# One decoder step on one core: compressed keys from token pairs on 128 rows, first scores between the two compressions, sums of a pair of units in one copy

## The chip, the cores and the metric

The kernel runs on one core of a Trainium2 chip. The metric is the device time of one execution in microseconds (us), the median of three runs; lower is better. A core has the engines PE (TensorE, matrix products), DVE (VectorE), ACT (ScalarE), POOL (GpSimd) and SP (SyncE, which here only issues DMAs). They run their own instruction streams and meet at semaphores.

## The reference, cut to what matters

One step of a hybrid decoder for 1024 prompt tokens and 8 samples of 4 tokens, each sample with 256 cached tokens. One of its three head groups is sparse attention, in which each query also looks at *compressed* keys and values. They are made like this:

```python
CMP_LEN, CMP_STRIDE, CMP_HIDDEN, HEAD_DIM = 32, 16, 128, 64

def nsa_compress(rows, w1, w2, pe):          # rows: (batch, tokens, 64)
    n_cmp = (rows.shape[1] - CMP_LEN) // CMP_STRIDE + 1
    idx = jnp.arange(n_cmp)[:, None] * CMP_STRIDE + jnp.arange(CMP_LEN)[None, :]
    blocks = rows[:, idx] + pe
    h = jax.nn.gelu(jnp.einsum('bnld,ldh->bnh', blocks, w1))
    return jnp.einsum('bnh,hd->bnd', h, w2)

kc = nsa_compress(nkv[:, :, 0], cw1[0], cw2[0], cpe[0])
vc = nsa_compress(nkv[:, :, 1], cw1[1], cw2[1], cpe[1])
```

A window is 32 tokens long and windows start every 16 tokens: 63 for the prompt, 15 for each sample. Keys and values go through the same two layers with their own weights. The prompt attention then adds four outputs for each head and block of 128 queries: fox (forgetting attention), slc (selected blocks, here all of them), win (a window of 512) and cmp (the compressed keys).

## The kernel before

All data are float32. Large products run first (stages p1 and hgrn, to about 475 us of the span). Stage p2b projects keys and values of the prompt tile by tile: a first loop over nine token tiles for fox (512 columns), then a second for the sparse heads (400 columns, `token_tile`, L709). In the second loop PE turns each finished tile (`turn_sparse_keys`, L807) and DVE copies the three turned blocks out of PSUM (`sparse_keys_turned`, L1733, L1734, L1736): 128 rows hold keys (rows 0 to 63) and values (64 to 127) of the compression as `kcvc`, with tokens along the columns. After the last tile PE turns the cached tokens of the samples (L826, four banks of four blocks), ACT copies them out (L1378), and PE turns the last tile and the position table (L834).

Stage p3 makes the compressed keys and values. PE makes 32 products for the keys and 32 for the values (L845), in turn on rows 0 to 63 and 64 to 127, one for each position l in the window; its moving operand is every 16th column of `kcvc` from l on, 193 columns. DVE adds the bias (L1794 to L1798) and makes the gelu over all 366 columns (L1779 to L1789) with one Exp on ACT (L1393). PE makes four second products (L850 to L860), DVE copies their results (L1802 to L1811); the last of these copies is the event "KC ready".

Beside it ACT makes the log forget values and copies the queries (L1385, L1389); after the event "LF ready" (L1767) POOL issues 15 DMAs of outputs (L2250 to L2258).

Stage attn runs over 64 units d: 4 heads, 8 query blocks i, and for each (fox, slc) as an even d and (win, cmp) as an odd one. Each engine has its own loop written out by hand:

- PE (L938): `scores(d)` (L887), `transposes(d-2)` (L899), `values(d-3)` (L911 and L912 for even units, L924 and L926 for odd). Ahead of it, and at every 16th unit, `decay_rows` (L869).
- DVE (L1882): `scores(d)` adds the bias and takes the least value (L1853), `normalise(d-1)` (L1863 to L1869), and at even d `add_halves(d-3)` (L1878), which frees the bank of the sums. `decay_rows` (L1826) is a chain of eight steps.
- ACT (L1406): copies of the turned probabilities of d-2 (L1419), then two Exps of unit d (L1428). At even d the sums of unit d-3 are copied between the two Exps: L1403 copies the lower half to `other_half`, L1404 the fox output to `QT`.
- POOL adds the diagonal mask for each head (`foxdiag`, L2264, L2267); the DVE `scores` of even units wait for it.

PSUM has eight banks: ring "vec" of four (scores and decay rows, in the order in which they are asked for), three for turned probabilities and one for the sums. SP's queue is in order too: bias strips of heads 0 and 1 (L525, L526), the first layer's weights `w1c` (L532, L533, after the wait for the first loop of p2b), the 16 cached pages `KVT` (L544), and after "KC ready" the rest of the caches (L549 on).

## Time and profile before

| what | value |
|---|---|
| median of three runs | 1415.16 us (1415.08 to 1419.33) |
| the profiled execution | 1417.93 us, of which the span of the page is 1416.1 us |
| PE busy | 1274.9 us, 90% of the span |
| DVE, ACT, POOL busy | 51%, 30%, 13% |
| mean granted clock of PE | 0.951 |

In the rows below "busy" is the time in which an engine's instructions ran, and "granted clock" the share of TensorE's full clock (1.00 is 2.4 GHz, 0.50 is 1.2 GHz). A float32 product is shown as two instructions ("x2"). The chain of waits is followed back from the last instruction to what released each step.

### The profile page before, as it was taken

The page shows a single profiled execution, that of the slowest core. Times are in us where ns is not written, and L with a number is a line of the kernel's source. Part 1 is how long each engine was busy: PE and PEld are TensorE (multiplying, and loading weights), DVE is VectorE, ACT ScalarE, POOL GpSimd, SP SyncE. Part 2 cuts the span into 40 slices and gives each one's busy share as a digit, 9 for nine tenths or more (in the row PEclk, how much of TensorE's full clock was granted, in tenths as well). Part 3 has the DMA queues.
Part 4 walks back from the last instruction along what each step waited for, and adds up shares of the span by engine and source line. Part 5 has one row for each costly group of instructions (what it writes and reads, how often), then busy time and mean ns, then how long its engine had stood idle before and what let it go on. Part 6 is the DMA issues. An engine that isn't in the chain of part 4 may idle for free.

```text
span 1416.1 us, 19719 instructions
## 1 busy us (share of the span) xinstructions
PE 1274.9 (90%) x6966; PEld 760.1 (54%) x6966; DVE 724.3 (51%) x1693; ACT 419.3 (30%) x894; POOL 177.6 (13%) x209
## 2 busy tenths in 40 slices
PE   3699999999999999969998999999829999999966
PEld 1468787787877545645665665545323333333322
DVE  5526584665755101247787783344752443433339
ACT  2232242422321200226666773222201111111016
POOL 0003121031221000200000000000001222211132
PEclk9799999999999999968999999999958999999988
DMA  9812021030111204204100005410267978495856
GB/s 314 246 31 60 2 66 25 23 70 3 31 60 47 98 0 90 96 6 121 42 18 24 16 1 164 153 45 15 82 232 244 321 240 296 151 334 158 283 181 224
DMA packets 124360, 163.19 MB, mean 115 GB/s; under 512 B 29860, under 2 KB 98644, under 8 KB 124281
## 3 DMA queue, kind: packets, MB, share of 16 engines
q1 hardware_dynamic: 109960, 112.75, 26.2%
q0 software_dynamic: 14320, 49.41, 10.2%
q8 instruction: 48, 0.79, 0.2%
q14 instruction: 32, 0.25, 0.1%
HBM read 225.01 MB, written 36.45 MB: 185 GB/s over the span
## 4 chain that ended last, share of the span: by engine, by line
PE 75%; DVE 15%; DMA 3%; ACT 3%; issue 2%; POOL 1%; SPq 0%; DVEq 0%; POOLq 0%; ACTq 0%
PE act L680 16%; PE vec L1202 11%; PE vec L962 9%; PE vec L709 7%; PE vec L730 4%; PE act L899 4%; PE vec L887 4%; DMA arena<-x_rows,arena 2%; PE act L911 2%; PE act L1215 2%; PE vec L1215 2%; PE vec L845 1%; PE act L924 1%; PE vec L690 1%; DVE arena L1653 1%
## 5 line engine op out<-in xcount | busy, mean ns | idle before, releaser
L680 PE MATMUL act<-arena 128*128 128x352 f32 x768 | 239.3, 468 | 0.4 <-issue 0.4
L680 PEld LDWEIGHTS act<-arena 128*128 128x128 f32 x768 | 145.7, 193 | 77.1 <-issue 3.7
L1202 PE MATMUL vec<-arena 128*64 128x512 f32 x768 | 173.8, 605 | 2.8 <-issue 2.8
L962 PE MATMUL vec<-arena 128*128 128x512 f32 (+1 forms) x288 | 126.6, 594 | 1.1 <-DVE arena L1878 1.1
L1202 PEld LDWEIGHTS vec<-arena 128*64 128x64 f32 x768 | 54.4, 138 | 105.3 <-issue 105.0
L709 PE MATMUL vec<-arena 128*128 128x512 f32 (+1 forms) x256 | 99.9, 546 | 0.0
L2157 DVE TENSOR_SCALAR arena<-arena 128x256 f32<-128x256 f32 x24 | 7.1, 295 | 172.5 <-ACT arena L1521 172.5
L1428 ACT ACTIVATE arena<-arena 128x640 f32<-128x640 f32 (+15 forms) x128 | 82.3, 645 | 20.6 <-DVE arena L1853 20.3
L962 PEld LDWEIGHTS vec<-arena 128*128 128x128 f32 (+1 forms) x288 | 50.9, 180 | 68.4 <-issue 66.1
L1419 ACT COPY arena<-act 128x512 f32<-128x512 f32 (+11 forms) x176 | 63.4, 428 | 62.1 <-PE act L899 62.0
L1853 DVE CUSTOM_DVE_ANT_0 arena<-vec,arena 128x128 f32<-128x128 f32 (+6 forms) x168 | 68.8, 430 | 24.5 <-PE vec L887 15.6
L899 PE MATMUL act<-arena 128*128 128x128 f32 (+4 forms) x440 | 67.0, 290 | 14.5 <-DVE arena L1869 13.9
L887 PE MATMUL vec<-arena 64*128 64x512 f32 (+11 forms) x376 | 72.5, 469 | 3.2 <-DVE arena L1853 2.0
L709 PEld LDWEIGHTS vec<-arena 128*128 128x128 f32 x256 | 47.8, 190 | 44.9 <-issue 27.7
L1674 DVE COPY_PREDICATED arena<-arena,vec 128x512 f32<-128x512 int32 x64 | 44.5, 728 | 48.3 <-PE vec L730 46.4
L899 PEld LDWEIGHTS act<-arena 128*128 128x128 f32 (+4 forms) x440 | 47.7, 143 | 36.0 <-DVE arena L1869 22.3
L730 PEld LDWEIGHTS vec<-arena 128*128 128x128 f32 x512 | 61.9, 192 | 9.3 <-DVE arena L1657 3.2
L690 PE MATMUL vec<-arena 128*128 128x128 f32 (+1 forms) x576 | 65.3, 275 | 0.0
L690 PEld LDWEIGHTS vec<-arena 128*128 128x128 f32 (+1 forms) x576 | 64.5, 183 | 1.3
L730 PE MATMUL vec<-arena 128*128 128x128 f32 x512 | 62.7, 276 | 2.4 <-DVE arena L1657 2.4
L1521 ACT ACTIVATE arena<-vec 128x256 f32<-128x256 f32 x24 | 9.3, 386 | 167.0 <-PE vec L1202 167.0
L1297 ACT ACTIVATE arena<-act,arena 128x352 f32<-128x352 f32 x36 | 20.0, 555 | 127.4 <-PE act L680 127.4
(383 smaller groups left out, 1940.5 us busy)
## 6 DMA issues: line engine op xcount, KB each, us to landing
arena<-in_exp_w SPq DMA_DIRECT2D x144, 1024.0 KB
y_rows<-arena POOLq DMA_DIRECT2D x48, 256.0 KB, 4.8
arena<-in_w_in SPq DMA_DIRECT2D x16, 512.0 KB, 6.8
arena<-in_x_prompt SPq DMA_DIRECT2D x8, 512.0 KB, 9.2
x_spill<-arena POOLq DMA_DIRECT2D x8, 512.0 KB, 5.3
arena<-x_spill SPq DMA_DIRECT2D x8, 512.0 KB, 5.1
arena<-in_cache_fox_kv SPq DMA_DIRECT2D x16, 256.0 KB, 3.5
x_rows<-arena POOLq DMA_DIRECT2D x8, 512.0 KB, 2.9
```

The costliest lines, as they stand in the source:

```text
L680: last = mm(bk[:, 0:n], W[k % 2][:, c, m * P:(m + 1) * P], xT[:, c, a:a + n], start=c == 0, stop=c == NC - 1)
L690: last = mm(bk[:r, o:o + P], xT[:, c, t * P:t * P + r], W[h % 2][:, c, 3 * P:4 * P], start=c == 0, stop=c == NC - 1)
L709: last = mm(bk[:r, 0:width], xT[:, c, t * P:t * P + r], w[:, c, 0:width], start=c == 0, stop=c == NC - 1)
L730: last = mm(bk[:, c * P:(c + 1) * P], a[:, ch], b[:, ch], start=True, stop=True)
L887: mm(bk[:, 0:n], q[s, h, i * P:(i + 1) * P], k[:, 0:n], start=True, stop=True).then_inc(*E.filled("vec", *events))
L899: last = e.transpose(bk[:n, c * P:(c + 1) * P], score_tiles(d)[j][:, (a + c) * P:(a + c) * P + n], ident)
L962: last = mm(bk[:r], src, Wo[half][:, c, :], start=c == 0, stop=c == NC - 1)
L1202: last = mm(gu_bank[p][o], xgT[p][:, c, o], Wgu[:, slot, c, :], start=c == 0, stop=c == NC - 1)
L1215: last = mm(dn_bank[half][o], hT[p][:, f, o], Wd[:, slot, f, half * 512:(half + 1) * 512], start=f == 0, stop=f == 1)
L1419: e.copy(turned_tiles(d)[j][:w, a:a + k, :], bk[:w, 0:k * P].rearrange("p (c n) -> p c n", c=k)).then_inc(*E.drained("turned", ("pt", d, j)))
L1428: act(s, s, ACT.Exp, scale=-1.0, bias=sm_[:, least(i, kind, j):least(i, kind, j) + 1], accum_out=sm_[:, j:j + 1]).then_inc(*E.done(("exps" ...
L1853: ins = e.tensor_tensor_reduce(out=out, in0=in0, in1=bias, scale=1.0, scalar=prior, op0=ALU.add, op1=ALU.min, accum_out=sm_[:, col + m[j]: ...
```

## The change

1. `kcvc` is replaced by `tokens2`: rows 0 to 63 hold even tokens, rows 64 to 127 odd ones, for keys and values apart, so that the windows of one offset lie in neighbouring columns. The first layer is 16 products for the keys and 16 for the values, each over 128 rows and 193 neighbouring columns. Each turned block is copied out in four pieces (keys and values, even and odd), by DVE for the prompt, by ACT for the cached tokens.
2. The cached tokens are turned inside the second loop of p2b, after tiles 1, 3, 5 and 7; the position table after tile 0.
3. Keys and values of the compression are worked apart. PE's order is: hidden layer of the keys, `decay_rows(0)`, scores of unit 0, hidden layer of the values, second layer of the keys (one product), scores of units 1 and 2, second layer of the values, and on. DVE and ACT have matching orders; the compressed keys are copied out by ACT.
4. The sums of an odd unit are one ACT copy of 128 rows straight to `QT`, and DVE adds the last part from PSUM. ACT makes this copy ahead of both Exps of unit d.
5. SP's order: long strips, cached pages, `w1c` in four DMAs, then, after the wait for the second loop of p2b, the local strips of heads 0 and 1. The later cache loads wait for "VC ready".

```diff
-    kcvc, KVT = zk.take(NTOK), zk.take(DB * PAST, DB, NP)
+    tokens2, KVT = zk.take(NTOK + DB * PAST, 2, 8), zk.take(DB * PAST, DB, NP)
...
@@ sync
         load_strips(0)
         load_strips(1)
-        e.wait_ge(*E.at(("w_in used", 5)))
-        e.dma_start(w1c[0:64], I["nsa_cmp_w1"][0, 0].rearrange("l d x -> d l x")).then_inc(*E.moved("cmp_in"))
-        e.dma_start(w1c[64:128], I["nsa_cmp_w1"][0, 1].rearrange("l d x -> d l x")).then_inc(*E.moved("cmp_in"))
...
         for n in range(DB * NP):
             e.dma_start(KVT[:, n // NP, n % NP, :], nkp[page_of(n), :, 0:2].rearrange("a p k d -> p (a k d)")).then_inc(*E.moved("cmp_cache_in"))
-        e.wait_ge(*E.at("KC ready"))
+        e.wait_ge(*E.at(("w_in used", 5)))
+        for kv in range(2):
+            for odd in range(2):
+                src = I["nsa_cmp_w1"][0, kv].rearrange("(j two) d x -> two d j x", two=2)
+                e.dma_start(w1c[64 * odd:64 * odd + 64, kv], src[odd]).then_inc(*E.moved(f"cmp{kv}_in"))
         e.wait_ge(*E.at(("w_in used", 6)))
+        load_local_strips(0)
+        load_local_strips(1)
+        e.wait_ge(*E.at("VC ready"))
@@ tensor
         for t in range(NT):
             token_tile(t, W_nkvg, 400, 6)
+            if t == 0:
+                e.wait_ge(*E.at("pe_in"))
...
+                e.wait_ge(*E.at("cmp_cache_in"))
+            if t % 2 and t < 8:
+                turn_cached_keys(t - 1)
             if t >= 2:
                 turn_sparse_keys(t - 2)
+        turn_sparse_keys(7)
...
+        e.wait_ge(*E.at("pairs by act"))
+        e.wait_ge(*E.at("cmp_in"))
+        def hidden_values(kv):
+            e.wait_ge(*E.at(f"cmp{kv}_in"))
+            e.wait_ge(*E.at(("pairs by vec", kv)))
+            e.wait_ge(*E.free("vec"))
+            bk = E.bank("vec")
+            for j in range(16):
+                last = mm(bk[:, 0:WINDOWS], w1c[:, kv, j, :], tokens2[:, kv, j % 8, j // 8:j // 8 + WINDOWS], start=j == 0, stop=j == 15)
+            last.then_inc(*E.filled("vec"))
...
-        for l in range(32):
-            for kv in range(2):
-                s = slice(64 * kv, 64 * kv + 64)
-                last = mm(hidden_banks[kv][:, 0:WINDOWS], w1c[s, l, :], skew(kcvc[s, :], l, [16, WINDOWS]), start=l == 0, stop=l == 31)
...
+        hidden_values(0)
+        e.wait_ge(*E.at("LF ready"))
+        decay_rows(0)
         E.stage("attn")
-        e.wait_ge(*E.at("KC ready"))
...
         for d in range(n + 3):
+            if d == 1:
+                hidden_values(1)
+                compressed_keys()
+                e.wait_ge(*E.at("KC ready"))
...
+            if d == 4:
+                e.wait_ge(*E.at("VC ready"))
...
+            if d == 2:
+                compressed_values()
@@ scalar
-        def lower_sums(d):
+        def sums(d):
             h, i, _ = PAIRS[d]
             e.wait_ge(*E.full("summed"))
             bk = E.job("summed")
-            e.copy(other_half[64:128], bk[0:64, P:2 * P]).then_inc(*E.done(("other half", d)))
-            e.copy(QT[0:64, h, i * P:(i + 1) * P], bk[0:64, 0:P]).then_inc(*E.done(("fox output", d)))
+            e.copy(QT[:, h, i * P:(i + 1) * P], bk[:, 0:P]).then_inc(*E.done(("sums copied", d)))
         for it in range(n + 3):
+            if it == 1:
+                compressed_keys()
+                gelu_exp(1)
...
+            if it >= 4 and it % 2 == 0:
+                sums(it - 3)
...
-                    if j and it >= 3 and kinds[0] == "fox":
-                        lower_sums(it - 3)
@@ vector
+        def pairs_of(bk, n, at):
+            for kv in range(2):
+                turned = bk[64 * kv:64 * kv + 64, 0:n].rearrange("p (w r two) -> p two r w", r=8, two=2)
+                for odd in range(2):
+                    last = cp(tokens2[64 * odd:64 * odd + 64, kv, :, at // 16:(at + n) // 16], turned[:, odd])
+                    last.then_inc(*E.done(*([("pairs by vec", kv)] if odd else [])))
...
-            cp(kcvc[:, t * P:(t + 1) * P], bk[:, 0:P]).then_inc(*E.done())
+            pairs_of(bk, P, t * P)
...
-            e.wait_ge(*E.at(("other half", d)))
-            e.wait_ge(*E.at(("fox output", d)))
-            tt(QT[64:128, h, i * P:(i + 1) * P], bk[64:128, 0:P], other_half[64:128], ALU.add).then_inc(*E.drained("summed", ("halves added", d), "prompt attention done"))
+            e.wait_ge(*E.at(("sums copied", d)))
+            x = QT[64:128, h, i * P:(i + 1) * P]
+            tt(x, x, bk[0:64, P:2 * P], ALU.add).then_inc(*E.drained("summed", ("halves added", d), "prompt attention done"))
         n = len(PAIRS)
+        gelu_inner(0)
         decay_rows(0)
+        gelu_outer(0)
         for it in range(n + 3):
+            if it == 1:
+                normalise(0)
+                gelu_inner(1)
             if it < n:
                 scores(it)
+                if it == 1:
+                    gelu_outer(1)
+                if it == 2:
+                    compressed_values()
```

`gelu_inner(kv)` and `gelu_outer(kv)` are the steps of the old gelu ahead of and behind its Exp, each for 183 of the 366 columns.

## Rows read from the trace of the kernel before

**Rows 1.** Chain of waits around stage p3: start us, us, what.
```profile
586.60 21.18 PE vec L845 x128
611.66 2.45 DVE arena L1787
624.46 2.00 POOL arena L2264
```

**Rows 2.** Ten-us stretches: length, busy PE, PEld, DVE, ACT, POOL, granted clock, DMA, GB/s.
```profile
610.00:620.00 10.00, 4.50 (x26) 3.79 (x27) 5.41 (x9) 0.51 (x1) 0.00 (x0) 0.50 0.00 0
630.00:640.00 10.00, 9.97 (x43) 5.31 (x40) 5.98 (x33) 5.80 (x24) 0.00 (x0) 0.50 0.09 9
```

**Rows 3.** Groups by form: busy us, mean ns of one, idle before.
```profile
L845 PE MATMUL vec<-arena 64*128 64x193 f32 x128 | 21.2, 501 | 0.9 <-DVE arena L1757 0.9
L709 PE MATMUL vec<-arena 128*128 128x400 f32 x112 | 38.6, 499 | 0.0
```

**Rows 4.** Timeline of the end of p2b: start us, us, engine, line, instruction.
```profile
583.24 1.91 PE L826 MATMUL act<-arena 128*128 128x128 f32 x16
582.99 1.12 DVE L1745 TENSOR_TENSOR arena<-vec,arena 32x100 f32<-32x100 f32 x4 [0.45 <-PE vec L699]
585.51 0.29 DVE L1733 COPY arena<-vec 128x128 f32<-128x128 f32 x1 [0.54 <-PE vec L807]
```

**Rows 5.** Timeline beside and behind the 193-column products, columns as in rows 4.
```profile
589.30 3.88 ACT L1389 COPY arena<-arena 64x1024 f32<-64x1024 f32 x4
590.18 0.94 POOL L2250 DMA_DIRECT2D out_new_fox_kv_p<-arena  x1 [133.96 <-DVE arena L1772]
595.20 3.99 POOL L2258 DMA_DIRECT2D out_new_nsa_win_s<-arena x8
607.80 0.16 DVE L1794 COPY arena<-vec 128x1 f32<-128x1 f32 x1 [17.43 <-PE vec L845]
615.45 0.23 DVE L1802 COPY arena<-vec 64x63 f32<-64x63 f32 x1 [0.78 <-PE vec L850]
616.47 1.89 PE L860 MATMUL vec<-arena 128*15 128x64 f32 x16
621.30 0.29 DVE L1826 TENSOR_SCALAR arena<-vec 128x128 f32<-128x128 f32 x1 [2.23 <-PE vec L869]
626.48 0.29 DVE L1853 CUSTOM_DVE_ANT_0 arena<-vec,arena 128x128 f32<-128x128 f32 x1 [2.12 <-POOL arena L2264]
```

**Rows 6.** The same units of heads 0 and 2: DVE scores(d=3), PE decay_rows at d=8.
```profile
630.19 0.28 DVE L1853 CUSTOM_DVE_ANT_0 arena<-vec,arena 128x128 f32<-128x128 f32 x1
647.75 2.05 PE L869 MATMUL vec<-arena 128*128 128x128 f32 x16 [0.71 <-DVE arena L1853]
...
752.14 0.29 DVE L1853 CUSTOM_DVE_ANT_0 arena<-vec,arena 128x128 f32<-128x128 f32 x1
765.16 2.05 PE L869 MATMUL vec<-arena 128*128 128x128 f32 x16 [0.77 <-DVE arena L1853]
```

**Rows 7.** Timeline of a short even unit (d=36), columns as in rows 4.
```profile
756.05 0.26 ACT L1404 COPY arena<-act 64x128 f32<-64x128 f32 x1
756.45 0.29 DVE L1878 TENSOR_TENSOR arena<-act,arena 64x128 f32<-64x128 f32 x1 [0.46 <-ACT arena L1404]
```

**Rows 8.** Timeline of the longest even unit (d=30), columns as in rows 4.
```profile
736.75 1.18 ACT L1428 ACTIVATE arena<-arena 128x1024 f32<-128x1024 f32 x1
737.28 0.27 PE L926 MATMUL act<-arena 128*64 128x128 f32 x1
738.49 1.15 ACT L1428 ACTIVATE arena<-arena 128x1024 f32<-128x1024 f32 x1
740.35 0.15 DVE L1863 SCALAR_TENSOR_TENSOR arena<-arena 128x2 f32<-128x2 f32 x1
742.22 2.00 PE L899 MATMUL act<-arena 128*128 128x128 f32 x16 [0.87 <-DVE arena L1869]
```

**Rows 9.** DMA issues of 480 to 640 us: count, KB each, median us to landing.
```profile
arena<-strip_rows SPq DMA_DIRECT2D x2, 320.0 KB, 6.5
```

More of the change, by code:

```diff
@@ L47 @@
 STRIPW = SLCW + WINW
[L48 removed]
+HALF_GELU = NCMP + DB * NCMPS
+GELU = 2 * HALF_GELU
 WINDOWS = NTOK // 16 + 16 * DB - 1
@@ L1377, in _ @@
             bk = E.job("act")
-            e.copy(KVT[:, b:b + 2].rearrange("p b j n -> p (b j n)"), bk).then_inc(*E.drained("act", "KVT ready"))
+            at = (NTOK + b * PAST) // 16
+            for kv in range(2):
+                turned = bk[64 * kv:64 * kv + 64].rearrange("p (w r two) -> p two r w", r=8, two=2)
+                for odd in range(2):
+                    last = e.copy(tokens2[64 * odd:64 * odd + 64, kv, :, at:at + PAST // 8], turned[:, odd])
+                    last.then_inc(*(E.drained("act", "pairs by act") if kv and odd else E.done()))
         e.wait_ge(*E.at("gate logits"))
@@ L1390, in _, with gelu_exp, compressed_keys @@
         E.stage("p3")
-        def gelu_exp(n, tag):
-            e.wait_ge(*E.at((tag, "inner")))
-            act(gu[:, 0:n], gu[:, 0:n], ACT.Exp, scale=-1.5957691216057308).then_inc(*E.done((tag, "exp")))
-        gelu_exp(GELU, "cmp hidden")
+        def gelu_exp(kv):
+            u = gu[:, kv * HALF_GELU:(kv + 1) * HALF_GELU]
+            e.wait_ge(*E.at(("gelu inner", kv)))
+            act(u, u, ACT.Exp, scale=-1.5957691216057308).then_inc(*E.done(("gelu exp", kv)))
+        def compressed_keys():
+            e.wait_ge(*E.full("act"))
+            bk = E.job("act")
+            e.copy(KC[64:128, 0:NCMP], bk[64:128, 0:NCMP]).then_inc(*E.done())
+            e.copy(KCs[64:128, :], bk[64:128, NCMP:HALF_GELU]).then_inc(*E.drained("act", "KC ready"))
+        gelu_exp(0)
         E.stage("attn")
         n = len(PAIRS)
-        def lower_sums(d):
+        def sums(d):
             h, i, _ = PAIRS[d]
@@ L1773, in _, with gelu_inner @@
         e.reciprocal(GT[:, 8, :], GT[:, 8, :]).then_inc(*E.done())
-        def gelu(n, tag):
-            x, u = gx[:, 0:n], gu[:, 0:n]
+        def gelu_inner(kv):
+            o = kv * HALF_GELU
+            x, u = gx[:, o:o + HALF_GELU], gu[:, o:o + HALF_GELU]
+            e.wait_ge(*E.full("vec"))
+            bk = E.job("vec")
+            cp(pc[:, kv:kv + 1], bk[:, 64:65]).then_inc(*E.done())
+            e.wait_ge(*E.own())
+            ts(x[:, 0:NCMP], bk[:, 0:NCMP], pc[:, kv:kv + 1], None, ALU.add).then_inc(*E.done())
+            sampled = skew(bk, 66, [16, DB], [1, NCMPS])
+            ts(x[:, NCMP:].rearrange("p (b n) -> p b n", b=DB), sampled, pc[:, kv:kv + 1], None, ALU.add).then_inc(*E.drained("vec"))
             e.wait_ge(*E.own())
```

130 lines of the change are left out of this document (59 added, 71 removed).

## The prediction

> **What bounds the kernel now.** I read the page first: PE is busy 90% of the span, so a microsecond taken out of PE's stream, or out of a wait of PE, is worth about a microsecond, and work of the other engines is worth something only where PE waits for it. Then the chain of waits, to see where PE does wait, around the part that the change touches [rows 1]. From 586.60 PE makes the first layer of the compression for 21.18 us; from 607.80 to the second layer DVE and ACT make the gelu with PE idle (the reciprocal alone is 2.45 us); then come decay rows and, last, a 2.00 us addition of POOL from 624.46. DVE makes the first scores only at 626.48 [rows 5]. So 586.60 to 626.48, 39.9 us, is one serial stretch. The ten-us stretches show its second price: the granted clock is 0.50 from 610 to 620, after PE had gone idle, and still 0.50 from 630 to 640, where PE is busy 9.97 of 10 us [rows 2]. Last the timelines of single units, to see whether the attention loop waits for the sums [rows 7, 8].
>
> I work with one point in both kernels: DVE's start on the scores of unit 3, at 630.19 now [rows 6]. Everything ahead of it is changed by parts 1 to 3 and 5 of the change; behind it only part 4 acts.
>
> **The first layer.** A 193-column product over 64 rows is recorded at 501 ns, as long as a 400-column product of neighbouring columns over 128 rows at 499 ns [rows 3]. 128 of the first take 21.2 us, 0.165 us each from start to start; 112 of the second took 38.6 us, 0.345 us each, 0.86 ns a column. The new layer has 64 instructions of 193 columns over 128 rows: at 0.86 ns a column 0.166 us each, 5.3 us for the keys and 5.3 us for the values. So 10.6 us of PE go, and this does not hang on why the old ones are long. Bounds: no row is below 0.86 ns a column, so it is no less; it would be 10.6 us a layer if a new product kept the 0.33 us that an old one needs for itself, should two of them run side by side. I take 5.3 because the 400-column row has the new form in everything but its length. The Trainium skill, SBUF — State Buffer, Specifications, says that memory lines are 16 bytes and that each step to a new line costs; the old operand steps 64 bytes, so the long recorded duration fits it. The Trainium skill, TensorE: Matmul & The Clock Gate, part 3 on packing small matmuls, says that products on different row groups run at the same time, so stacking on 128 rows would bring nothing by itself. By both together the old pairs ran side by side at half rate and the new time is the same 10.6 us; by the second alone, had the stride been free, it would have been no gain.
>
> **The end of p2b.** Turning the cached tokens (1.91 us on PE) moves ahead of the last tile; PE's total stays, so PE has nothing left at about 585.6, as now. But DVE now does the last work. Its additions for the sample tile (1.12 us, now from 582.99) follow PE's products for it, which come 1.9 us later with the turning ahead of them, so they run from 585.0 to 586.1 [rows 4]. Behind them come the copies of two turned blocks; each was three copies and is six. A copy of 64x63 out of PSUM took 0.23 us, one of 128x128 0.29 us [rows 4, 5], so four of 64x64 for one of 128x128 add 0.6 us, and a block is about 1.45 us. The keys of the last block lie ready at 586.1 + 1.45 + 0.45 = 588.0, where the products of now begin at 586.60: +1.4 us. The pieces are read out of PSUM in steps of 16 columns; no row has that form. Between free and double the time the +1.4 is -0.4 (if the pieces are hidden behind PE) to +3.0; I take the row's price. The Trainium skill, PSUM — Partial Sum Buffer, Specifications, says that PSUM lines are 8 bytes and that an access that isn't contiguous slows matmuls; should that hold for copies too, the upper bound and a sum 1.6 us higher would be right. ACT's part, four copies of 64x256 a bank, is spread over four tiles; the last is due about 3 us before it is wanted. DVE's last copies end at 589.0, some 2.2 us later than now, and "LF ready", which stands behind them on DVE and ACT, shifts with them.
>
> **The order behind it.** PE makes the keys' layer from 588.0 to 593.4 and then the decay rows, but may not start scores before ACT has copied the queries: 3.88 us from 589.30 now [rows 5], so until about 595.5. DVE: bias and the first half of the gelu for 183 instead of 366 columns, 593.5 to 595.1; ACT's Exp 597.1; the decay chain 3.1 us (621.30 to 624.46 now) to 598.2; the outer half, half of a 2.45 us reciprocal [rows 1] and two short steps, 1.85 us, to 600.1. But the first scores of DVE also wait for POOL, and POOL is the late one: it issues 15 DMAs, from 590.18 to 599.19 now, 9.0 us [rows 5], released by "LF ready", now 2.2 us later. So 592.4 to 601.4, then its 2.00 us addition [rows 1], and DVE starts the first scores at **603.5** instead of 626.48: -23.0 us. Today those DMAs lie beside the 21 us of products and cost nothing; that cover is gone. The Trainium skill, SBUF — State Buffer, "Who interferes with whom", says that VectorE and GpSimd share a port pair under an exclusive lock; the DMA issues, which run while DVE idles now, would then be stretched by those of DVE's steps that read and write SBUF, about 1 us of them (an estimate), and the sum would be 1 us higher.
>
> **Between the first scores and unit 3.** What was ahead of the loop is now in it. After the scores of unit 0 at 604.0 come ACT's two Exps (to 604.8), DVE's normalise (to 605.6), `gelu_inner(1)` 1.5 us, scores 1 0.5 us, `gelu_outer(1)` 1.8 us to 609.5, scores 2 1.1 us. PE has made the values' layer from 596.7 (when a bank of the decay rows is drained) to 602.1 and the keys' second product, all before 603, so both are hidden; it then waits for ACT's copy of the keys (605.4, queued behind the Exps of unit 0) with scores 1, and for `gelu_outer(1)` at 609.5 with the values' second layer, 0.4 + 1.89 us at half clock [rows 5]. DVE's copy of it ends at 612.5, normalise(1) at 613.3: scores 3 start at **613.3** instead of 630.19. Sum of parts 1 to 3 and 5: **-16.9 us**. Of the 23.0, 6.1 are given back here; if POOL or DVE are late ahead of it, the same is added.
>
> **SP's queue.** The pages move ahead by some 50 us; `w1c` waits for the first loop of p2b as now and is due at 588, a whole loop later; the local strips are issued at 585, take 6.5 us [rows 9] and are due at 603.5 with the first scores. All are covered by 12 us or more. Were that cover gone, each us late would be a us. The later cache loads wait for "VC ready", some 5 us sooner than now, and are wanted only behind the attention loop.
>
> **The clock.** PE is busy perhaps a third of 602 to 613, no more than in the stretch that now keeps 0.50 (4.50 of 10 us from 610 to 620 [rows 2]), so I expect 0.50 from about 605 and its return at the same unit as now. What a full clock would be worth is read from equal work: from scores 3 to the decay rows at unit 8 head 0 takes 630.19 to 647.75, 17.6 us, head 2 takes 752.14 to 765.16, 13.0 us, though it also finishes the head before [rows 6]. That is 4.5 us more if the clock stays up.
>
> **The sums.** Two ACT copies of 64x128, 0.26 us each, become one of 128x128 (0.25 to 0.3 us). ACT has 32 of each, 8.5 us less work beside PE. On the path it counts only where DVE waits for them: at a short unit DVE waits 0.46 us for the second copy, ending 756.31 [rows 7], and the copy will now stand ahead of the Exps and be done by then. The chain of waits runs over the second copy at 7 places of this kind, two or three at each change of heads: 7 x 0.42 = 2.9 us, and 0.3 at the end of the loop for the copy that is gone: **-3.2 us**. Against it: ACT now stands with both Exps behind it until PE has made `values(d-3)`. At the longest unit the first Exp starts at 736.75 and PE's values end at 737.55; with the copy it will start at 737.9, and the second, which ends at 739.64 now, at 740.25. DVE gets to its normalise at 740.35, and PE waits 0.87 us for it [rows 8]. That is no loss, with 0.1 us to spare. Bounds for this part: 0.5 us lost at each of 12 long units is +6, the full 0.46 us at all 16 places where DVE now waits is -7; I take the chain's own count.
>
> **The sum.** 1417.93 - 16.9 - 3.2 = 1397.8 for the profiled execution; that lies 2.8 us above the median of the three runs, so 1415.16 - 20.1 = **1395.0 us** for the median.
>
> **The rivals.**
> - *The clock stays up* through the start of attention: another -4.5 us, 1390. [...] 15%.
> - *The wait for the sums costs*: ACT's later Exps reach PE at the middle and long units, +6 instead of -3.2: 1404. For it speaks that at the longest unit only 0.1 us is spare [rows 8]; against it that PE has 1 us in hand in most others. 12%.
> - *The products are not shortened* (the change doesn't do what it says): a new product keeps 330 ns, so each layer takes 10.6 us. DVE's chain ends 5.3 us later, 605.4 against POOL's 603.5, and PE comes to the keys' second product only at 612.7 instead of 602: with the overlap of the two, +8 us, 1403. Against it stands the 400-column row [rows 3]. 5%.
> - *Slower*: ACT's wait ahead of both Exps reaches the path at every even unit. The price is 0.6 us of a later second Exp, more where PE's values are longer; 32 units at 0.66 us are 21 us and use up the 16.9 gained by more than 4: 1419 and up. It decides from 0.66 us a unit. Against it: where PE is the bound it is 9 to 10 us busy in 10 with the Exps in its shadow. 2%.
> - *Nothing gained in sum* (the same, with 0.5 us a unit): 1%.
> - The forecast: 65%.
>
> **Range and chances.** 1386 to 1404 takes in the clock (-4.5), the ends of the tail of p2b (-1.8, +1.6), POOL's port (+1), and a part of either end of the sums; it leaves out about 15%. Faster by over 0.3% (about what a measurement of this kernel can tell from no change) 0.97, within 0.3% 0.01, slower by over 0.3% 0.02.
>
> **What would show it.** The 193-column products at about 330 ns and 5.3 us a layer; PE's gap ahead of them 2.4 us; POOL's addition as what releases the first scores at 603.5; scores 3 at 613; the granted clock 0.50 from about 605 to 625; no waits of DVE for ACT's sums in the short units, and the second Exp of long units 0.6 us later with PE's 0.87 us wait unchanged. The prediction is wrong if the first scores wait for DVE's chain or the strips instead, if the copies out of PSUM are far longer than 0.23 us, or if PE waits at long units for more than 0.87 us.

## The result and the profile after

The changed kernel takes **1397.7 us** (1396.33 to 1399.13) beside 1417.05 us (1415.08 to 1419.33) of the kernel before on the same chip: ratio 0.985, 95% interval 0.983 to 0.987, so 1.3 to 1.7% less. The prediction said 1395.0, in a range of 1386 to 1404. In a second comparison the changed kernel took 1398.17 beside 1417.86 (0.9855, 0.9837 to 0.9873). The profiled execution took 1398.77 us.

The head of its page: PE's busy time fell from 1274.9 to 1262.4 us, 12.5 us, and the span by 19.2 us. The rest of the span's fall is PE's idle time, not its work.

```profile
span 1396.9 us, 19607 instructions
PE 1262.4 (90%) x6900; PEld 757.3 (54%) x6900; DVE 732.2 (52%) x1724; ACT 413.5 (30%) x877; POOL 177.4 (13%) x209
```

Groups by form, 560 to 620 us: the new product and its yardstick.

```profile
L717 PE MATMUL vec<-arena 128*128 128x400 f32 x68 | 23.7, 499 | 0.0
L856 PE MATMUL vec<-arena 128*128 128x193 f32 x64 | 11.0, 328 | 3.8 <-DVE arena L1775 2.6 <-DVE arena L1874 1.2
```

A 193-column product is now recorded at 328 ns on average instead of 501 [rows 3]; the 64 instructions take 11.0 us, where 128 took 21.2.

The chain of waits (start us, us, what) shows what took the place of the 21 us of [rows 1]: DVE's log forget values release POOL's output DMAs, these and POOL's addition end last, and the first scores follow.

```profile
594.78 0.30 DVE arena L1822 x2
595.09 0.94 POOL out_new_fox_kv_p L2307
...
600.10 3.98 POOL out_new_nsa_win_s L2315 x8
604.10 2.13 POOL arena L2321
606.25 0.31 DVE arena L1901 x2
```

DVE's timeline beside it (start us, us, engine, line, instruction, idle before and releaser): the tail of p2b, DVE's last step of the gelu, its wait for POOL, and the scores of unit 3.

```profile
588.51 0.98 DVE L1775 COPY arena<-vec 64x64 f32<-64x64 f32 x4
589.94 0.98 DVE L1775 COPY arena<-vec 64x64 f32<-64x64 f32 x4
...
602.89 1.48 DVE L1852 TENSOR_TENSOR arena<-arena 128x183 f32<-128x183 f32 x1
606.25 0.29 DVE L1901 CUSTOM_DVE_ANT_0 arena<-vec,arena 128x128 f32<-128x128 f32 x1 [1.89 <-POOL arena L2321]
...
612.12 0.35 DVE L1852 TENSOR_TENSOR arena<-arena 128x183 f32<-128x183 f32 x1
614.85 0.68 DVE L1860 COPY arena<-vec 15x512 f32<-15x512 f32 x1 [1.31 <-PE vec L874]
616.17 0.28 DVE L1901 CUSTOM_DVE_ANT_0 arena<-vec,arena 128x128 f32<-128x128 f32 x1
```

PE's timeline: both layers, and what it waits for ahead of each step.

```profile
590.66 5.48 PE L856 MATMUL vec<-arena 128*128 128x193 f32 x32 [2.57 <-DVE arena L1775]
599.88 5.48 PE L856 MATMUL vec<-arena 128*128 128x193 f32 x32 [1.20 <-DVE arena L1874]
607.91 0.78 PE L901 MATMUL vec<-arena 64*128 64x128 f32 x6 [2.23 <-ACT arena L1432]
612.53 0.47 PE L870 MATMUL vec<-arena 128*63 128x64 f32 x2 [2.40 <-DVE arena L1852]
612.93 1.89 PE L874 MATMUL vec<-arena 128*15 128x64 f32 x16
```

Ten-us stretches, columns as in [rows 2]: the sixth number after the length is the granted clock. It is about half from 610 to 620 only, while the kernel before was still at 0.50 from 630 to 640.

```profile
600.00:610.00 10.00, 7.38 (x44) 6.40 (x44) 6.99 (x22) 1.24 (x6) 6.20 (x10) 1.00 0.79 238
610.00:620.00 10.00, 7.06 (x40) 4.55 (x38) 6.86 (x33) 3.94 (x18) 0.00 (x0) 0.52 0.02 1
620.00:630.00 10.00, 9.49 (x69) 5.72 (x67) 8.89 (x41) 7.47 (x26) 0.00 (x0) 0.97 0.07 4
```

**A ledger of milestones.** Stage p2b starts at different times in executions whose code up to there is the same (474.8 to 478.9 us over the 14 executions profiled here; 475.84 before, 478.08 after), so each milestone below is counted from PE's first product of p2b in its own trace. The differences are taken ahead of rounding.

| us from the start of p2b to | before | after | difference | forecast |
|---|---|---|---|---|
| first product of the layer | 110.8 | 112.6 | +1.8 | +1.4 |
| DVE's first scores | 150.6 | 128.2 | -22.5 | -23.0 |
| DVE's scores 3 | 154.4 | 138.1 | -16.3 | -16.9 |
| PE's decay rows of head 1 | 171.9 | 152.2 | -19.7 | -16.9 |
| first product behind the attention (L988) | 386.0 | 362.6 | -23.4 | -20.1 |
| end | 940.3 | 918.8 | -21.5 | -20.1 |

Between scores 3 and the decay rows of head 1 the kernel gains 3.5 us that the forecast had not: there the granted clock is higher than before. From there to the end of attention it gains 3.6 us (214.1 to 210.4); in this stretch the two differ by the sums alone. Behind attention 1.9 us are lost and ahead of p2b 2.2, in code that is the same in both. There the granted clock is a little lower, in long stretches of the changed kernel (0.98 in both; the kernel before has 0.99 and 1.00):

```profile
100.00:470.00 370.00, 362.84 (x2054) 285.15 (x2053) 218.18 (x292) 114.89 (x147) 69.61 (x52) 0.98 0.14 37
870.00:950.00 80.00, 79.23 (x469) 40.53 (x468) 33.21 (x81) 19.39 (x41) 2.14 (x4) 0.98 0.21 72
```

The first of these goes with the execution, not with the kernel: of the 14 executions profiled here, the six with 0.99 in the first stretch start p2b at 474.8 to 477.5 us and the eight with 0.98 at 478.1 to 478.9, and two kernels that were profiled twice (`e2_no_sums` and `g2_no_sums_again`, `f4_sums_between` and `g3_sums_between_again`) lie once in each group. Behind attention the last of these pairs took 553.9 and 556.0 us, so a difference of 2 us arises there without any change of the kernel too.

### The profile page after: what moved, and what is told of

It is laid out like the page before. It is cut to its first block, busy times and chain, and to the rows that moved or that the text cites. A ratio compares the mean times of both kernels' runs of the same rounds, so it can differ in the third digit from the quotient of the medians.

```text
span 1396.9 us, 19607 instructions
## 1 busy us (share of the span) xinstructions
PE 1262.4 (90%) x6900; PEld 757.3 (54%) x6900; DVE 732.2 (52%) x1724; ACT 413.5 (30%) x877; POOL 177.4 (13%) x209
## 4 chain that ended last, share of the span: by engine, by line
PE 73%; DVE 16%; DMA 3%; issue 3%; ACT 2%; POOL 1%; SPq 0%; DVEq 0%; POOLq 0%; ACTq 0%
PE act L688 16%; PE vec L1228 11%; PE vec L988 9%; PE vec L717 7%; PE vec L738 4%; PE act L913 4%; PE vec L901 3%; DMA arena<-x_rows,arena 2%; PE act L1241 2%; PE vec L1241 2%; PE act L925 2%; PE act L938 1%; PE vec L698 1%; DVE arena L1901 1%; DVE arena L1917 1%
## 5 line engine op out<-in xcount | busy, mean ns | idle before, releaser
L988 PE MATMUL vec<-arena 128*128 128x512 f32 (+1 forms) x288 | 128.3, 600 | 0.8 <-DVE arena L1926 0.8
L988 PEld LDWEIGHTS vec<-arena 128*128 128x128 f32 (+1 forms) x288 | 51.5, 182 | 69.2 <-issue 67.2
L1693 DVE TENSOR_TENSOR arena<-arena 128x512 f32<-128x512 f32 (+1 forms) x28 | 28.4, 1014 | 55.7 <-PE vec L738 55.7
```

The lines of the kernel that those rows point to most:

```text
L988: last = mm(bk[:r], src, Wo[half][:, c, :], start=c == 0, stop=c == NC - 1)
```

## The experiments

### The stride and the stacking of rows

Two kernels made from the one before touch only the old first layer. `e3_neighbours` reads 193 neighbouring columns in place of every 16th:

```diff
-                last = mm(hidden_banks[kv][:, 0:WINDOWS], w1c[s, l, :], skew(kcvc[s, :], l, [16, WINDOWS]), start=l == 0, stop=l == 31)
+                last = mm(hidden_banks[kv][:, 0:WINDOWS], w1c[s, l, :], kcvc[s, l:l + WINDOWS], start=l == 0, stop=l == 31)
```

> The kernel before with the 64 products of the first layer reading 193 neighbouring columns instead of every 16th (it computes other hidden values; the count, the sizes and the turns between rows 0 to 63 and 64 to 127 are kept). Theory that the old pairs ran side by side at half rate because of the stride: recorded 0.327 us each and about 0.083 us from start to start, so the layer takes 10.6 instead of 21.2 us and the kernel is 10 us shorter, with no stacking on 128 rows at all. Rival that the old products ran one after the other and the stride cost nothing: 21.2 us again, no change.

`e4_apart` keeps the stride but makes all 32 products of the keys ahead of all 32 of the values, so that neighbours in time share a row group:

```diff
-        for l in range(32):
-            for kv in range(2):
+        for kv in range(2):
+            for l in range(32):
```

> The kernel before with all 32 products of the keys ahead of all 32 of the values, strided operands kept, so that neighbours in the stream use the same rows. Theory that the old pairs ran side by side at half rate: 0.33 us from start to start, the layer takes about 42 us instead of 21.2, the kernel is 21 us longer. Rival (one after the other, no cost of the stride): 21.2 us again, no change.

Groups by form of `e3_neighbours`, then of `e4_apart` (busy us, mean ns of one):

```profile
L845 PE MATMUL vec<-arena 64*128 64x193 f32 x128 | 10.7, 324 | 0.9 <-DVE arena L1757 0.9
```

```profile
L845 PE MATMUL vec<-arena 64*128 64x193 f32 x128 | 40.9, 502 | 0.9 <-DVE arena L1757 0.9
```

With neighbouring columns the old layer takes 10.7 us instead of 21.2, at 324 ns an instruction instead of 501. That is as short as the new layer (11.0 us), which has half as many products on twice the rows. So the whole of the gain in PE's time is that of the columns; the stacking on 128 rows by itself brings nothing. `e4_apart` shows why: with the row groups no longer in turn the same 128 instructions take 40.9 us, so the old pairs had run side by side.

The clock could have made those 40.9 us as well, because most of them passed at half the clock:

```profile
585.00:590.00 5.00, 4.40 (x14) 3.02 (x15) 2.12 (x16) 3.86 (x7) 0.81 (x1) 0.93 0.00 0
600.00:610.00 10.00, 10.00 (x35) 9.40 (x35) 0.00 (x0) 0.00 (x0) 0.00 (x0) 0.50 0.20 34
```

The starts in the trace rule that out. Before the clock fell, at 589.3, the instructions of `e4_apart` were 0.326 us apart behind the first few, and from 590 to 600, at 0.50, they were 0.327 us apart. These strided products went no faster at the full clock. The same rows show that the clock can be at 0.50 while PE is recorded as busy 10.00 of 10 us, so it isn't found only where PE has gaps; why it fell there is open.

In its milestones `e3_neighbours` has the first scores 10.3 us sooner than before (140.3 us from the start of p2b), which is about the layer's own gain of 10.5; it took 1405.84 us in one run, `e4_apart` 1435.86.

What the changed kernel has beyond `e3_neighbours` ahead of the first scores is 140.3 - 128.2 = 12.1 us. The timelines point to the work apart, since the first scores need only the keys' half of layer and gelu, but no run has this part alone.

### The sums

`e1_sums_only` is the kernel before with part 4 alone, `e2_no_sums` the changed kernel without it. The edit, as a part of the first:

```diff
-            e.copy(other_half[64:128], bk[0:64, P:2 * P]).then_inc(*E.done(("other half", d)))
-            e.copy(QT[0:64, h, i * P:(i + 1) * P], bk[0:64, 0:P]).then_inc(*E.done(("fox output", d)))
+            e.copy(QT[:, h, i * P:(i + 1) * P], bk[:, 0:P]).then_inc(*E.done(("sums copied", d)))
...
+            if it >= 4 and it % 2 == 0:
+                sums(it - 3)
...
-                    if j and it >= 3 and kinds[0] == "fox":
-                        lower_sums(it - 3)
```

> The kernel before with part 4 of the change alone (one copy of 128 rows for the sums, ahead of both Exps). Theory: -3.2 us against before (1413 to 1415 beside 1417), all of it at the units round a change of heads, DVE's waits for ACT's sums (17.9 us in 16 places before) nearly gone, PE's wait of 0.87 us at the longest unit unchanged. Rival: ACT, held up by PE's values with both Exps behind it, gives +3 to +6 us at the middle and long units, seen as PE waiting for the normalise there.

> The changed kernel with part 4 taken back (two copies of 64 rows, between the Exps). Theory: the other parts are worth -16 to -20 us by themselves, so about 1400, some 3 us above the changed kernel. The stretch from the start of p2b to the decay rows of head 1 should be 19.8 us shorter than before, as in the changed kernel. Rival: the parts help each other, then this one and the sums alone don't add up to the change (difference over 3 us).

`e1_sums_only` took 1413.39 us beside 1417.13 (ratio 0.9972, 0.9958 to 0.9986): 2.0 to 6.0 us less. `e2_no_sums` took 1398.93 (0.9885, 0.986 to 0.9911), above the changed kernel in ratio but with intervals that overlap. The gains of the two, 3.7 and 18.2 us, make 21.9 where the changed kernel has 19.4, within the 3 us that the expectation allowed. From the decay rows of head 1 to the end of attention the traces take 214.1 us before and 208.6 with part 4 alone; 215.7 without part 4 and 210.4 with it in the changed kernel: 5.5 and 5.2 us. Is it the place of the copy or its count? `f4_sums_between` is the changed kernel with the single copy at the old place:

```diff
-            if it >= 4 and it % 2 == 0:
-                sums(it - 3)
...
                 for j, kind in enumerate(kinds):
+                    if j and it >= 3 and kinds[0] == "fox":
+                        sums(it - 3)
```

> The changed kernel with one edit: the single copy of the sums (128x128, 0.27 us) stands again between ACT's two Exps of a unit instead of ahead of them, for every unit rather than for two at a time. It tells what the 5.2 us of part 4 come from. Theory (the place: with the copy ahead of the Exps DVE's addition of the halves no longer waits for it, and fewer and wider copies matter little beside it): the time is 2 to 4 us above the changed kernel, near that of e2_no_sums (1398.9, where the two copies stand at their old places), and DVE's waits for the copy, 17.9 us in 16 places before and 6.2 in 2 now, are back. Rival (the count: ACT works 8.5 us less, wherever the copy stands): the same time as the changed kernel within 1 us.

It took 1395.37 us beside 1418.11 (0.9842, 0.9824 to 0.986), no more than the changed kernel, and 209.4 us over the same stretch. The theory of the expectation (the place) fell. Since this and `e2_no_sums` came from different comparisons, three kernels ran once more beside each other:

> The changed kernel itself, to stand beside the other three, since their differences are of a few us and the median of one kernel moves by about 2 us from one comparison to the next. Expected 1396 to 1398.

> The changed kernel without part 4 (two copies of the sums between the Exps, DVE's addition from two SBUF tiles), beside the changed kernel. If part 4 is worth what the traces of the attention stage show (215.6 us from the decay rows to the output projection against 210.5), it is 3 to 5 us slower than the changed kernel. Rival: part of that was the clock's short dips, and the difference is under 1.5 us.

> The changed kernel with the single copy between the two Exps, beside the two ends of part 4. Its trace of f4_sums_between took 209.4 us over the same stretch, as short as that of the changed kernel: if the count of the copies and not their place is what counts, it is within 1 us of the changed kernel and 3 to 5 us ahead of the one without part 4. Rival (the place counts): it lies with the kernel without part 4.

| kernel | median us | ratio, 95% interval | decay rows of head 1 to end of attention |
|---|---|---|---|
| g1_after_again | 1398.17 | 0.9855 (0.9837 to 0.9873) | 210.4 |
| g2_no_sums_again | 1403.05 | 0.9886 (0.9868 to 0.9903) | 215.7 |
| g3_sums_between_again | 1396.02 | 0.9836 (0.9821 to 0.9852) | 209.4 |

The stretch repeats within 0.1 us for each of the three, but not for one attention loop in different kernels: with two copies it took 214.0 to 215.7 us in five traces, with one copy ahead of the Exps 208.6 to 210.6 in seven. Two copies made one, with DVE's addition out of PSUM that goes with it, are worth 6.3 us at the old place in this comparison (4.6 by the nearest of the five), and the medians agree: the intervals of `g2_no_sums_again` and `g3_sums_between_again` don't meet. The place can't be priced: 209.4 lies among the seven, and the intervals of `g1_after_again` and `g3_sums_between_again` overlap. It gave nothing that shows. The groups of DVE's addition (busy us, mean ns, idle before it and releasers), without part 4, with the copy between, and in the changed kernel:

```profile
L1930 DVE TENSOR_TENSOR arena<-act,arena 64x128 f32<-64x128 f32 x32 | 9.4, 295 | 25.2 <-ACT arena L1444 17.2 <-PE vec L902 4.5 <-PE act L914 3.1
```

```profile
L1928 DVE TENSOR_TENSOR arena<-arena,act 64x128 f32<-64x128 f32 x32 | 9.1, 283 | 15.1 <-PE vec L901 7.5 <-ACT arena L1442 6.5
```

```profile
L1926 DVE TENSOR_TENSOR arena<-arena,act 64x128 f32<-64x128 f32 x32 | 9.1, 284 | 14.6 <-PE vec L901 7.5 <-ACT arena L1442 6.2
```

The wait for ACT goes from 17.2 us to 6.5 with one copy at the old place (6.9 in the second trace), and the move takes off a few tenths only. One short unit shows how, first with two copies (`e2_no_sums`), then with one between (`f4_sums_between`), timelines as above:

```profile
737.02 0.63 ACT L1473 ACTIVATE arena<-arena 128x384 f32<-128x384 f32 x1
737.77 0.26 ACT L1443 COPY arena<-act 64x128 f32<-64x128 f32 x1
738.05 0.26 ACT L1444 COPY arena<-act 64x128 f32<-64x128 f32 x1
738.44 0.29 DVE L1930 TENSOR_TENSOR arena<-act,arena 64x128 f32<-64x128 f32 x1 [0.47 <-ACT arena L1444]
```

```profile
736.02 0.63 ACT L1471 ACTIVATE arena<-arena 128x384 f32<-128x384 f32 x1
736.63 0.26 ACT L1442 COPY arena<-act 128x128 f32<-128x128 f32 x1
736.77 0.63 ACT L1471 ACTIVATE arena<-arena 128x384 f32<-128x384 f32 x1
737.00 0.28 DVE L1928 TENSOR_TENSOR arena<-arena,act 64x128 f32<-64x128 f32 x1
```

With two, the second ends 1.29 us after the Exp began and DVE waits 0.47 us; with one it ends at 0.87 us, and DVE, then busy with its normalise, finds it done. The second Exp gains too: it starts 0.75 us behind the first (736.77), where with two copies it starts 1.19 us behind (738.21).

### What the first scores wait for

`f1_outputs_early` takes POOL's output DMAs out from behind "LF ready", all but two:

```diff
         e.wait_ge(*E.at("fkv ready"))
-        e.wait_ge(*E.at("nkvg ready"))
-        e.wait_ge(*E.at("LF ready"))
         e.dma_start(O_["new_fox_kv_p"][0, 0].rearrange("(t p) k h d -> p t (k h d)", p=P), fkv).then_inc(*E.moved("kv_out"))
...
+        e.wait_ge(*E.at("nkvg ready"))
...
+        e.wait_ge(*E.at("LF ready"))
+        e.dma_start(O_["new_fox_logf_p"][0, 0].rearrange("(t p) h -> p t h", p=P), LF[:, 0:8, :]).then_inc(*E.moved("kv_out"))
```

> The changed kernel with one edit: POOL issues the output DMAs of keys and values as soon as each is ready, and only the two of the decay logarithms behind "LF ready" (in the changed kernel all stand behind it, 595.1 to 604.1, and POOL's addition from 604.10 is what releases DVE's first scores at 606.25). Theory (POOL's queue sets the first scores, as the prediction's step on the order has it): POOL reaches its addition when DVE's decay chain is done, at about 601.5, and the first scores start at 603.3 to 604.0, so 2.3 to 3 us earlier; the 1.48 us addition of DVE at 602.89 (0.35 us where POOL issues nothing) shortens as well. The time falls by 2 to 3 us against the changed kernel, to about 1395. Rival (DVE's own chain of the gelu is as late as POOL): the first scores move by less than 1 us and the time does not change. Second rival (it is given back by scores 3, where the values' second layer and the copy of the keys set the time): first scores 603.5, scores 3 still near 616, time unchanged.

Its first scores start at 605.24, 126.7 us from the start of p2b: 1.5 us sooner, not 2.3 to 3. Its median is 1395.36 us (0.9844, 0.9819 to 0.9868), which can't be told from the changed kernel's. POOL is now released by DVE's decay chain (first row), which stands behind the first half of the gelu. In this execution PE's layer for the keys met a stretch of lower clock (0.66 from 590 to 595, second row) and took 6.92 us instead of 5.48; without these 1.4 us the first scores would have come 2.9 us sooner (an estimate), as expected:

```profile
603.12 1.99 POOL L2321 TENSOR_TENSOR arena<-arena 128x1024 f32<-128x1024 f32 x1 [6.22 <-DVE arena L1874]
```

```profile
590.00:595.00 5.00, 3.92 (x15) 3.95 (x16) 2.65 (x17) 2.55 (x6) 5.00 (x11) 0.66 1.00 330
```

The start was lost again behind that: the decay rows of head 1 came 154.4 us after the start of p2b, 2.2 us later than in the changed kernel, with a granted clock of 0.59 from 620 to 630, where the changed kernel has 0.97.

`f2_both` also puts the sample tile's additions behind the last copies of turned blocks, with PE's turns in the same order:

```diff
-                sparse_keys_turned(t - 2)
                 continue
...
             if t >= 2:
                 sparse_keys_turned(t - 2)
-        sparse_keys_turned(7)
+            if t == 7:
+                sparse_keys_turned(6)
+                sparse_keys_turned(7)
```

> The edit of f1_outputs_early and one more: in the second loop of the stage before, the sample tile's additions come last on DVE, and the copies of the last two turned blocks and PE's turns stand ahead of them. Theory (the tail of that stage costs 1.4 us in the changed kernel because DVE's additions and the six copies of a block follow PE's last products): PE's gap ahead of the new layer falls from 2.6 us to about 1.2 us, the layer starts 1.4 us sooner, and with POOL out of the way DVE's first scores follow: 1.4 us sooner than in f1_outputs_early, so about 1393.5. Rival ("LF ready", which stands behind the sample tile's additions on DVE and ACT, holds the decay chain): the layer starts sooner but the first scores do not, and the time is that of f1_outputs_early.

PE's gap ahead of the layer falls from 2.57 to 1.44 us, and the first scores start at 602.57, 124.2 us from the start of p2b: 4.0 us sooner than in the changed kernel. But of this 0.7 us is left at the decay rows of head 1 (151.5 instead of 152.2), and the median is 1395.44 us (0.9834, 0.9814 to 0.9855). The stretches of `f2_both` show the clock low from 607.6 to 624.6, 17 us, in the changed kernel only for 10 us from 610.4 on (the expectation of `g4_all` below puts the 17 us at 601 to 618, which these rows don't bear out):

```profile
605.00:610.00 5.00, 2.68 (x20) 1.99 (x21) 4.51 (x19) 2.11 (x11) 0.00 (x0) 0.76 0.00 0
610.00:615.00 5.00, 4.46 (x27) 2.78 (x24) 2.96 (x15) 1.77 (x9) 0.00 (x0) 0.50 0.03 2
615.00:620.00 5.00, 5.00 (x21) 2.91 (x19) 3.03 (x16) 2.35 (x8) 0.00 (x0) 0.50 0.06 3
620.00:625.00 5.00, 5.00 (x22) 2.66 (x22) 2.81 (x16) 2.16 (x8) 0.00 (x0) 0.54 0.07 2
```

### The clock

`f3_filler` leaves the changed kernel as it is and gives PE five products of 512 columns more, where it waits. What they write is overwritten by the next product into the same bank.

```diff
+        def filler(bk, count):
+            for _ in range(count):
+                mm(bk[:, 0:512], w1c[:, 0, 0, :], w1c[:, 1, 0:4, :], start=True, stop=True)
...
                 compressed_keys()
+                e.wait_ge(*E.free("act"))
+                filler(banks["act"][(E.jobs["act"] + 1) % 4], 3)
...
             if d == 2:
+                filler(banks["summed"][0], 2)
                 compressed_values()
```

> The changed kernel with five extra 512-column products of PE whose results are overwritten: three ahead of PE's wait for the copy of the keys (about 605 to 608), two ahead of the second layer of the values. Theory (the clock of 0.50 from 610.2 to 620.4 in the changed kernel follows from PE's idle time in 602 to 616): the stretch of 0.50 is shorter or gone, and up to half of 10 us of PE's busy time comes back, 2 to 4 us; the extra products lie in idle time and cost nothing. Rival (other engines set the pace until scores 3, so that a full clock there speeds nothing, or the fillers are too few and their 0.44 us each at full clock or 0.87 at half are added): the same time or up to 2 us more, with 0.50 still there.

Its clock stays at 1.00 through the start of attention; the timeline has the second fill and the values' second layer, 1.07 us instead of 1.89:

```profile
610.00:615.00 5.00, 4.05 (x31) 2.45 (x30) 4.36 (x18) 2.55 (x11) 0.00 (x0) 1.00 0.01 3
615.00:620.00 5.00, 4.04 (x27) 2.38 (x27) 4.49 (x25) 2.83 (x12) 0.00 (x0) 1.00 0.05 3
```

```profile
610.30 1.88 PE L945 MATMUL act<-arena 128*128 128x512 f32 x4
613.12 1.07 PE L874 MATMUL vec<-arena 128*15 128x64 f32 x16
```

The decay rows of head 1 come 149.8 us after the start of p2b instead of 152.2 and the end of attention 359.6 instead of 362.6: 2.4 and 3.0 us. The median, 1396.17 us (0.9849, 0.9829 to 0.9868), can't be told from that of the changed kernel: 3 us are within what these intervals leave open.

If the clock is what took back the earlier start of `f2_both`, the start must be worth more with the five products in place. That is `g4_all`, `f2_both` with the same five products:

> f2_both with the five extra products of f3_filler. In f2_both the first scores came 3.6 us sooner than in the changed kernel, but the clock stood at 0.50 from about 601 to 618, 17.1 us instead of 10.2, and decay rows of head 1 were only 0.4 us sooner. Theory (the earlier start was given back through the clock, not through another engine): with the fillers the clock stays at 1.00 there, and the decay rows of head 1 come 3.5 to 5 us sooner than in the changed kernel (630.25), at 625.5 to 626.8; the time is 3 to 5 us below it. Rival (DVE's order between first scores and scores 3 takes the start back whatever the clock): decay rows of head 1 at about 628.2 as with the fillers alone, the time 2 to 3 us below the changed kernel.

```profile
600.00:610.00 10.00, 9.04 (x54) 5.34 (x52) 7.16 (x32) 3.34 (x15) 0.00 (x0) 1.00 0.00 0
610.00:620.00 10.00, 9.48 (x73) 5.84 (x71) 9.12 (x47) 7.45 (x27) 0.00 (x0) 1.00 0.07 5
```

**1389.1 us** (1388.19 to 1392.3), ratio 0.9804 (0.979 to 0.9818), clear of the interval of the changed kernel beside it (0.9837 to 0.9873): the fastest kernel of this case. From the start of p2b it needs 124.2 us to the first scores, 147.3 to the decay rows of head 1 (changed kernel 152.2, `f2_both` 151.5, `f3_filler` 149.8) and 357.9 to the end of attention (362.6, 362.0, 359.6). So 0.6 and 3.0 us apart, 4.7 together. The theory had 3.5 to 5 us at the decay rows, and it is 4.9. With the clock at 1.00 in both, the earlier start is worth 149.8 - 147.3 = 2.5 us there; without the five products 0.7 us of it were left. That 0.7 is one trace, not a fixed price: at this milestone two traces of one kernel, `f4_sums_between` and `g3_sums_between_again`, lie 2.7 us apart.

The five products aren't free, though. DVE now waits for PE with the scores of unit 1, behind the first fill:

```profile
604.24 0.29 DVE L1911 CUSTOM_DVE_ANT_0 arena<-vec,arena 128x128 f32<-128x128 f32 x1 [1.32 <-PE vec L903]
```

Scores 3 come 134.6 us after the start of p2b, in `f2_both` 134.1; only behind them does the full clock pay. A shorter first fill was not tried.

The medians of `g4_all` and of the changed kernel beside it are 9.1 us apart, the spans of their profiled executions 9.6. Of these 4.5 lie between the start of p2b and the end of attention, where the edits are; 3.5 lie ahead of it and 1.6 behind, where the code is the same and the granted clock was 0.99 and 1.00 in place of 0.98. Some of the 9 us is therefore a matter of these executions, and how much the medians owe to it is open.

## Why the prediction was right

Point by point, by its own steps.

- **The first layer: right.** The 64 instructions took 11.0 us where 10.6 was said, by the 400-column row [rows 3]. That old pairs had run side by side at half rate, which was only argued from the Trainium skill (SBUF — State Buffer, Specifications, on memory lines; TensorE: Matmul & The Clock Gate, part 3), is shown by `e3_neighbours` and `e4_apart`: 10.7, 21.2 and 40.9 us. The rival "not shortened" is out.
- **The end of p2b: right to 0.4 us.** PE's gap is 2.57 us (said 2.4). The four pieces of 64x64 took 0.98 us, 0.25 each, where 0.23 was said from the 64x63 copy of [rows 5]: the steps of 16 columns in PSUM cost a copy little or nothing. Here the rule of the Trainium skill (PSUM — Partial Sum Buffer, Specifications) would have added 1.6 us, if it held for copies as well, and the measurement speaks against that.
- **The order behind it: right.** POOL was the late one. From its first DMA (595.09) to its addition (604.10) it took 9.0 us as said, and the first scores are 22.5 us sooner, said 23.0. `f2_both` shows that with POOL's outputs out of the way and the layer 1.3 us sooner they come another 4.0 us sooner, at which point DVE's own chain is as late as POOL.
- **Shared port: an effect is there, on the other engine.** The prediction, by the Trainium skill (SBUF — State Buffer, "Who interferes with whom"), had DVE's steps stretch POOL's DMA issues by 1 us; the last eight of these took 3.99 us as before [rows 5]. It was a step of DVE that ran long. L1852, an elementwise step with both operands in SBUF, took 1.48 us beside POOL's last issues and 0.35 us at 612.12, and it did so in all five traces that have this order. It isn't so for every such step: two others of the same form (L1837 at 596.94, L1841 at 597.80) took 0.35 us each with POOL issuing all the while, and what sets the one apart is open. Beside POOL's addition the case is plainer. Where it had begun before DVE's step, in five traces, the step ended 0.2 us after the addition, and took 0.76 or 2.20 us by when it had started. Here from `g2_no_sums_again`:

```profile
605.01 2.01 POOL L2325 TENSOR_TENSOR arena<-arena 128x1024 f32<-128x1024 f32 x1
605.04 2.20 DVE L1856 TENSOR_TENSOR arena<-arena 128x183 f32<-128x183 f32 x1
```

In the changed kernel DVE had 1.89 us to spare behind the step, so it cost nothing.
- **Between first scores and scores 3: right.** 9.9 us from one to the other in the trace (606.25 to 616.17), said 9.8.
- **SP's queue: right.** Nothing in the stretch waits for it.
- **The clock: half right.** It fell, but at 610.4 and not from about 605 as said, and it came back at 620.7, not at the same unit as before. This is the step that failed: I gave the old kernel's low stretches (30.7 us at 0.50 between 608.6 and 642.7) to the new one because 602 to 613 looked as idle. PE was busy 6.0 of these 11 us in the changed kernel and not a third of them, and 7.1 of the ten us from 610 to 620, where the kernel before has 4.5 [rows 2]; that is all the traces tell of why. It is worth the 3.5 us in the ledger between scores 3 and the decay rows of head 1; that a higher clock there gives microseconds is shown by `f3_filler`. The rival "the clock stays up" (-4.5 us) didn't happen, but three quarters of its size came. Nor was it a term that could be fixed more closely: the same kernel, profiled as `f4_sums_between` and `g3_sums_between_again`, needed 152.0 and 154.7 us from the start of p2b to the decay rows of head 1, with a granted clock of 0.94 and of 0.71 from 620 to 630.
- **The sums: size near, reason wrong.** -3.6 us before against after, said -3.2; -5.2 and -5.5 by taking part 4 away or making it alone. I took it from the place, "the copy will now stand ahead of the Exps and be done by then". It is the count that gives it, together with DVE's addition out of PSUM, which no run takes apart from it: with the one copy at the old place the gain is all there, and the move takes only a few tenths off DVE's wait. The rival "the wait for the sums costs" (+6 instead of -3.2) is out; whether the move costs 1 us or nothing isn't told apart.
- **What no step had.** +2.2 us ahead of p2b and +1.9 behind attention, with a lower granted clock in code that didn't change. Without them the 23.4 us of the ledger would have made 1393.7 of the median of 1417.05. That 20.1 us were forecast and 19.4 measured is in part luck: these 4.1 us stand against the 3.5 that the clock gave at the start of attention. The rest of the distance from 1395.0 to 1397.7 is the kernel before, whose median was 1415.16 when I added up and 1417.05 here.

## What to carry to other kernels

- A recorded duration that is long for its columns, and a rate that looks right all the same, can be two effects that cancel. Changing one operand's stride, and the order of the row groups, tells them apart in two runs; only the stride was worth anything here.
- When a long stretch of one engine is cut, look at the in-order queue beside it that used to be covered: here 15 DMA issues of POOL set the new end. Where that is taken out as well, look at the clock: an earlier start was worth 0.6 us by the end of attention, keeping PE busy 3.0, and both 4.7, in one trace each.
- Two small copies made one at the same place gave the whole gain, and a cleverer place nothing that could be told from zero. Measure the edit and its place apart before you keep both.

## What the runs showed of the hardware

- An instruction with a float32 moving operand of 193 columns in steps of 64 bytes took 501 ns as recorded (64 rows), in neighbouring columns 324 ns (64 rows) and 328 ns (128 rows).
- Float32 products on rows 0 to 63 and 64 to 127 in turn ran side by side: 0.083 us an instruction (10.7 us for 128) against 0.172 us (11.0 for 64) on 128 rows; with the stride 0.166 us in turn and 0.32 us one group after the other (40.9 for 128).
- The strided products of one row group were 0.33 us apart at a granted clock of 1.00 and of 0.50 (`e4_apart`).
- The granted clock was 0.50 from 600 to 610 in `e4_apart` with PE recorded as busy 10.00 of the 10 us.
- A DVE step with both operands in SBUF that started beside POOL's addition ended 0.2 us after it (0.76 and 2.20 us instead of 0.35). Beside POOL's DMA issues one such step took 1.48 us and two took 0.35; the issues were not stretched.
- Five products in PE's waiting time (2.74 and 1.88 us as recorded) went with a granted clock of 1.00 from 600 to 630, where it had been near 0.50 for ten us; in `g4_all` the scores of unit 1 came 1.4 us later than in `f2_both`, in `f3_filler` no later than in the changed kernel.
